# Slabs on two sets of PSUM banks, with the other stages laid into them, in a decoder block on one core

## Chip, core and metric

One NeuronCore of a Trainium2 chip. The metric is device time in microseconds (us) of one execution; lower is better. TensorE does matmuls and transposes into PSUM (eight banks of 128 x 512 f32), ScalarE and VectorE read PSUM, GpSimdE works on SBUF and issues the gathers, SyncE issues the other loads.

## What is computed

One layer, 256 tokens (two blocks of 128), width 2048, all in f32:

```python
h = rmsnorm(x, norm1_w)
q, k, vr, gr, pin, gates = split(h @ w_in)             # 1024, 1024, 2048, 2048, 1024, 4096 columns
ret = silu(gr) * groupnorm(retention(rotary(q), rotary(k), vr))
pooled = (multiscale_pool(pin) @ w_pool_lin) * pool_scale
mixed = sigmoid(gates[0]) * (ret @ w_ret_o) + sigmoid(gates[1]) * (pooled @ w_pool_o)
x = x + mixed @ w_out
h2 = rmsnorm(x, norm2_w)
s = (h2 @ w_q) . sub_keys                              # 8 heads x 2 x 128 keys
# top 16 of each half, top 16 of their 256 sums: 16 experts of 16384 a head and token
a = u[expert] . h2 ; y = sum(gelu(a) * softmax(best) * v[expert])
out = rmsnorm(x + y, final_norm_w)
```

## The kernel before

**Slabs.** All big products run as 19 slabs of 1024 output columns for 256 tokens: 7 of w_in for the mixers (`S_MIX` 0 to 6), 4 for the gates (`S_GATE` 7 to 10), then two each for w_ret_o (`S_RET`), w_pool_o (`S_POOL`), w_out (`S_OUT`) and w_q (`S_Q`). A slab has 16 tiles of 128 rows of weights (8 in `S_POOL`), 288 in all. To keep f32 precision each tile and each activation is split into a high fp32r part and a low rest: SyncE loads `w_raw` (`slab_tiles`, L357), ScalarE rounds it to `w_hi` (`tiles`, L663), VectorE subtracts to `w_lo` (L877), and TensorE does three matmuls for each of four banks (L430 to L432), twelve a tile. `w_raw`, `w_hi` and `w_lo` are rings of `W_RING` = 4 tiles; ScalarE and VectorE run `LEAD` = 3 tiles ahead.

**PSUM.** All slabs write the same four banks, `bank`. The other four, `misc`, serve everything else. So the first matmul of a slab waits (`bank_free`) for the eviction of the slab before it: ScalarE evicts the mix slabs (L706), the gates (L745) and q (L771), VectorE the others (L972, L978, L986). A slab ends with a `drain`.

**What stands between slabs.** Each product needs its activations with the model dimension on partitions. `turn` (L439 to L450) does this in 32 transposes of 128 x 128, in eight groups, through `misc`; each group is evicted as a high part by ScalarE (L678) and a low part by VectorE (L886). `turn` runs four times, each time as a block ahead of a slab: stage 0 ahead of slab 0, on x times norm1_w (L913); stage 1 ahead of `S_RET`; stage 2 ahead of `S_OUT`; stage 3 ahead of `S_Q`, on h2 = x times norm2_w (L991). Between slab 6 and the gates stand the retention (L460 to L491) and the pooling (L497 to L511).

**First gate slab.** Beside it VectorE takes the group norm's statistics (L942, L945) and 16 normalisations in one piece (L956), ScalarE the silu, with fixed numbers of tiles between these blocks (`EARLY` = 4). GpSimdE multiplies (L1210), and later adds the two branches of `mixed` (L1217).

**Keys and top-k.** Behind each `S_Q` slab q is evicted (L771), transposed (L541), split again (L776, L998) and multiplied with the keys (L551 to L553, 24 matmuls for each token block); ScalarE copies the scores (L781). `top_experts(u)` (L1027 to L1059) finds the 16 experts of unit u, one of 16 units (token block and head), on VectorE. `next_tile` (L1023) puts a tile of the second `S_Q` slab between its steps and between the first dot products.

**Experts.** The upper half of each u row is gathered: GpSimdE issues 256 indirect loads of 512 KB (L1235, ring of four), VectorE multiplies each with h2 (`dot_product`, L1066), with `top_experts` of the later units and `q_low(1)` (L998) at fixed places between them. The lower half is done densely: SyncE streams all of u's lower half (L391), TensorE multiplies it in 128 keys of 16 matmuls (L568), ScalarE copies it to `plane` (L800), and later the entries wanted are picked from it by one-hot matmuls (L585, L593) and VectorE (L1128). These picks begin in the middle of the dots: `softmax_and_picks` (L1101) is called before dot 213. Then come the weights, their spreading to the dense keys (L625), the dense product with v's lower half (L641) beside 256 gathers of v's upper half that VectorE adds (L1152), and the final norm.

The order on each engine is the order in which the code issues it; semaphores tie the engines together. Most slabs are hardware loops (`Fori`).

## Time and profile before

| | us |
|---|---|
| median of 3 runs | 2248.27 (2241.54 to 2249.14) |
| span of the profiled execution | 2236.2 |
| TensorE matmuls busy | 2010.6 (90%) |
| VectorE busy | 1359.9 (61%) |
| ScalarE busy | 785.5 (35%) |
| GpSimdE busy | 759.5 (34%) |
| chain that ended last | PE 40%, DMA 25%, DVE 16%, issue 9% |

```profile
PE   6999999899999988899999988179876999999993
PEclk9999999999999999899999999689877899999997
DMA  6766662466564545889989899855677899999996
```

Each digit is a fortieth of the span, 55.9 us, in tenths. PE, PEld, DVE, ACT, POOL and SP are TensorE's matmuls, its weight loads, VectorE, ScalarE, GpSimdE and SyncE; the chip's record of the granted TensorE clock is in tenths of full speed. Matmul records overlap, since a matmul's record holds its tail: the pace is read from start to start. The slabs fill slices 1 to 16, the dense dots slices 17 to 25, the picks and the spreading slices 26 to 32, the dense product with v the rest.

### The profile page before, as it was taken

The numbers are of one execution on the slowest core, as the hardware profiler recorded it, in microseconds if no ns is written. First come the engines' busy times: TensorE is split into PE (matmuls) and PEld (weight loads), VectorE is DVE, ScalarE is ACT, GpSimd is POOL, SyncE is SP. The second block draws the span as 40 slices with busy tenths as digits, with TensorE's granted clock in tenths as the row PEclk, the third lists the DMA queues.
The fourth block names the chain that finished last, engine by engine and source line by source line (L and its number), as shares of the span: only waits on it lengthen the run. The fifth ranks groups of instructions, "written<-read, shape, count | busy, mean of one in ns | idle before, by whom it ended". The sixth has DMA issues, their size and how long they took to land.

```text
span 2236.2 us, 30445 instructions
## 1 busy us (share of the span) xinstructions
PE 2010.6 (90%) x8262; PEld 1515.3 (68%) x8262; DVE 1359.9 (61%) x2570; ACT 785.5 (35%) x1409; POOL 759.5 (34%) x642
## 2 busy tenths in 40 slices
PE   6999999899999988899999988179876999999993
PEld 5878887688787877788888877168765544444441
DVE  4554443644455455876776755579999655554556
ACT  4444445444434353211111111089899411111111
POOL 0340000100002001344443455578654554555453
PEclk9999999999999999899999999689877899999997
DMA  6766662466564545889989899855677899999996
GB/s 214 245 186 189 189 191 61 157 191 188 169 205 155 191 146 163 292 314 327 335 310 320 314 359 342 288 174 173 209 230 226 283 358 371 363 369 355 369 370 220
DMA packets 173711, 565.12 MB, mean 253 GB/s; under 512 B 19296, under 2 KB 20960, under 8 KB 172512
## 3 DMA queue, kind: packets, MB, share of 16 engines
q1 hardware_dynamic: 99936, 296.14, 39.9%
q0 software_dynamic: 73728, 268.47, 34.7%
q8 instruction: 16, 0.26, 0.0%
q14 instruction: 31, 0.25, 0.0%
HBM read 562.43 MB, written 2.10 MB: 252 GB/s over the span
## 4 chain that ended last, share of the span: by engine, by line
PE 40%; DMA 25%; DVE 16%; issue 9%; ACT 5%; POOL 3%; ACTq 0%; POOLq 0%; DVEq 0%; SPq 0%
DMA v_room<-in_peer_v_up,idx 14%; DMA v_room<-in_peer_u_up,idx 11%; PE bank L430 11%; PE bank L431 10%; PE bank L432 10%; DVE v_room L1066 4%; PE misc L593 4%; DVE x_sb L1152 2%; ACT qk_tmp L806 2%; POOL v_room L1235 2%; PE misc L625 2%; DVE w_lo L877 1%; ACT qk_tmp L811 1%; DVE qk_tmp L1012 1%; PE misc L585 1%
## 5 line engine op out<-in xcount | busy, mean ns | idle before, releaser
L877 DVE TENSOR_TENSOR w_lo<-w_raw,w_hi 128x1024 fp32r<-128x1024 f32 x288 | 370.1, 1288 | 385.8 <-ACT w_hi L663 385.2
L663 ACT ACTIVATE w_hi<-w_raw 128x1024 fp32r<-128x1024 f32 x288 | 305.0, 1060 | 466.8 <-PE bank L432 432.5
L1152 DVE SCALAR_TENSOR_TENSOR x_sb<-v_room,weight,x_sb 128x1024 f32<-128x1024 f32 x256 | 328.3, 1283 | 220.4 <-DMA v_room<-in_peer_v_up,idx 217.2
L430 PE MATMUL bank<-w_hi,act_hi 128*128 128x512 f32 x1088 | 428.8, 394 | 28.5 <-DVE w_lo L877 13.4
L641 PE MATMUL bank<-h,qk_tmp 128*128 128x512 f32 x1024 | 439.6, 592 | 0.0
L431 PE MATMUL bank<-w_lo,act_hi 128*128 128x512 f32 x1088 | 426.0, 392 | 0.0
L432 PE MATMUL bank<-w_hi,act_lo 128*128 128x512 f32 x1088 | 425.8, 391 | 0.0
L1066 DVE CUSTOM_DVE_ANT_0 v_room<-v_room,h 128x1024 f32<-128x1024 f32 x256 | 310.2, 1224 | 179.9 <-DMA v_room<-in_peer_u_up,idx 178.4
L1235 POOL DMA_INDIRECT v_room<-in_peer_u_up,idx x256 | 308.2, 1204 | 326.2 <-DVE dots_now L1066 264.2
L1235 POOL DMA_INDIRECT v_room<-in_peer_v_up,idx x256 | 303.9, 1187 | 309.6 <-DVE x_sb L1152 264.1
L641 PEld LDWEIGHTS bank<-h,qk_tmp 128*128 128x128 f32 x1024 | 194.6, 190 | 244.9 <-issue 244.9
L568 PE MATMUL bank<-final_w,h 128*128 128x256 f32 x1280 | 289.2, 383 | 15.3 <-DMA h<-in_peer_u_low 15.2
L568 PEld LDWEIGHTS bank<-final_w,h 128*128 128x128 f32 x1280 | 241.7, 191 | 58.6 <-DMA h<-in_peer_u_low 19.8
L430 PEld LDWEIGHTS bank<-w_hi,act_hi 128*128 128x128 f32 x1088 | 206.0, 189 | 77.8 <-DVE w_lo L877 14.7
L432 PEld LDWEIGHTS bank<-w_hi,act_lo 128*128 128x128 f32 x1088 | 205.9, 189 | 43.5
L431 PEld LDWEIGHTS bank<-w_lo,act_hi 128*128 128x128 f32 x1088 | 206.2, 189 | 42.2
L800 ACT ACTIVATE plane<-bank 128x256 f32 x128 | 49.2, 384 | 414.7 <-PE bank L568 384.0
L855 ACT ACTIVATE qk_tmp<-plane 128x256 f32 x128 | 53.3, 419 | 375.8 <-PE bank L641 366.5
L568 PE MATMUL bank<-final_w,t_extra 128*128 128x256 f32 x768 | 169.7, 379 | 0.0
L568 PEld LDWEIGHTS bank<-final_w,t_extra 128*128 128x128 f32 x768 | 145.9, 190 | 19.8
L625 PE MATMUL misc<-probs_picks,qk_tmp 128*128 128x128 f32 x512 | 107.2, 375 | 43.5 <-ACT qk_tmp L811 41.1
L625 PEld LDWEIGHTS misc<-probs_picks,qk_tmp 128*128 128x128 f32 x512 | 91.9, 270 | 58.9 <-ACT qk_tmp L811 55.9
(167 smaller groups left out, 1565.2 us busy)
## 6 DMA issues: line engine op xcount, KB each, us to landing
w_raw<-in_w_in SPq DMA_DIRECT2D x176, 512.0 KB, 3.6
h<-in_peer_v SPq DMA_DIRECT2D x128, 512.0 KB
h<-in_peer_u_low SPq DMA_DIRECT2D x160, 256.0 KB
t_extra<-in_peer_u_low SPq DMA_DIRECT2D x96, 256.0 KB
w_raw<-in_w_ret_o SPq DMA_DIRECT2D x32, 512.0 KB, 3.8
w_raw<-in_w_out SPq DMA_DIRECT2D x32, 512.0 KB, 3.7
w_raw<-in_peer_w_q SPq DMA_DIRECT2D x32, 512.0 KB, 3.8
w_raw<-in_w_pool_o SPq DMA_DIRECT2D x16, 512.0 KB, 4.7
```

The lines of the kernel that those rows point to most:

```text
L430: pe.matmul(o, lh, rh, start=(k == 0), stop=False)
L431: pe.matmul(o, lh, rl, start=False, stop=False)
L432: m = pe.matmul(o, ll, rh, start=False, stop=(k == kc - 1))
L568: m = pe.matmul(bank[:, n, 0:SEQ], t_ring[r][:, k * P:(k + 1) * P], h2_t[:, s * LOW_KC // 2 + k, :], start=(s == 0 and k == 0), stop=(s == ...
L593: i = pe.matmul(misc[:, 2 + m, n * P:(n + 1) * P], keys_t[:, m, n * P:(n + 1) * P], plane[:, :, bass.ds(g * GROUP + n, 1)].rearrange("p k ...
L625: m = pe.matmul(misc[:, q, n * P:(n + 1) * P], second_hot[:, q % 2, n * P:(n + 1) * P], first_hot[:, q % 2, n, :], start=True, stop=True)
L641: m = pe.matmul(bank[:, 2 * b + h, :], staged[:, r, b * P:(b + 1) * P], e_ring[:, r, h * HALF:(h + 1) * HALF], start=False, stop=False, sk ...
L663: act.activation(w_hi[:, r, :], w_raw[:, r, :], ACT.Copy).then_inc(tile_hi, 1)
L877: dve.tensor_tensor(w_lo[:, r, :], w_raw[:, r, :], w_hi[:, r, :].bitcast(F32), ALU.subtract)\
L1066: dve.tensor_tensor_reduce(out=g_ring[:, r, :], in0=g_ring[:, r, :], in1=h2[:, b, HALF_D:D], scale=1.0, scalar=0.0, op0=ALU.mult, op1=ALU.add,
L1152: dve.scalar_tensor_tensor(acc, g_ring[:, r, :], weight[:, bass.ds(u, 1), k:k + 1].rearrange("p u k -> p (u k)"), acc, ALU.mult, ALU.add). ...
L1235: pool.indirect_dma_start(out=g_ring[:, r, :], out_offset=None, in_=table, in_offset=bass.IndirectOffsetOnAxis(ap=idx[:, m, k:k + 1], axis=0),
```

## The change

- `bank` and `misc` become two equal sets of four banks. Slab s writes `sets[set_of(s)]`, in turn, and waits for that set alone (`set_free[0]`, `set_free[1]` instead of `bank_free`). A set that is free in between takes transposes. The `drain` goes: ScalarE waits for `bank_full` of the slab before it refills the ring slot of the slab's last tile.
- The transposes of all four stages go into slabs, a group of four transposes between one or two tiles. A group now holds two 128-blocks of columns for both token blocks, as the contraction wants them, and a tile waits only for its own group. Stage 0 and 3 transpose x itself; norm1_w and norm2_w, transposed once by TensorE into `norm_t`, are multiplied in as the evictions' scale. x comes in two loads.
- In the first gate slab tiles stand between each two steps of the statistics and the normalisation on VectorE and between the silus on ScalarE.
- The adds of the two branches move from GpSimdE to VectorE, into the evictions of the `S_POOL` slabs (`mix`).
- The first `S_Q` slab's q is transposed after three tiles of the second, its keys are scored after six and seven; top-k of unit 0 starts in that slab. The second slab's q is transposed after two dense keys and scored after eight. `q_low(1)` moves from behind the 15th to behind the 13th dot.
- Constants load one by one between tiles of slab 1; the rotation's table goes ahead. All slab loops are unrolled.

The core of the diff, with the same helpers for ScalarE and VectorE left out where they mirror TensorE's order:

```diff
+def set_of(slab):
+    return (slab + (slab >= S_GATE)) % 2
...
         def _(sp):
-            sp.dma_start(x_sb[:, :, :], a["x"].rearrange("(t p) d -> p t d", p=P)).then_inc(x_landed, 16)
-            sp.dma_start(norm1, a["norm1_w"].rearrange("(o d) -> o d", o=1).to_broadcast([P, D])).then_inc(norm1_landed, 16)
+            sp.dma_start(x_sb[:, :, 0:SLAB], x_rows[:, :, 0:SLAB]).then_inc(x_landed, 16)
...
+            slab_tiles(a["w_in"], 0, 0, 0, LEAD)
+            sp.dma_start(x_sb[:, :, SLAB:D], x_rows[:, :, SLAB:D]).then_inc(x_rest_landed, 16)
...
+            def slab(s, k0, k1, hi, lo):
+                out_set, n, t0, kc = sets[set_of(s)], uses_before(s), first_tile(s), tiles_of(s)
...
                             if k == 0:
-                                pe.wait_ge(bank_free, 4 * s + b + 1)
-                            o = bank[:, b, :]
+                                pe.wait_ge(set_free[set_of(s)], 4 * n + b + 1)
+                            o = out_set[:, b, :]
...
-                    (pe.drain() if k == kc - 1 else m).then_inc(split_free, 1)
+                    if k < kc - 1:
+                        m.then_inc(split_free, 1)
...
+            turn(0, x_sb, misc)
+            turn(1, x_sb, misc)
+            for g in range(8):
+                act_slab(0, 0, 2 * g, 2 * g + 2)
...
+                    turn(g + 2, x_sb, misc)
...
+            for g in range(8):
+                slab(S_RET - 1, 2 * g, 2 * g + 2, act_hi, act_lo)
...
+                turn(g, ret_rows, bank)
+            for b in range(BANKS):
+                pe.wait_ge(turned_lo, 8 + 4 + b + 1)
+            act_slab(S_RET, 1, 0, KC)
...
+            slab(S_POOL + 1, 0, 4, pact_hi, pact_lo)
+            pe.wait_ge(mixed_ready, BANKS)
+            for g in range(4):
+                turn(g, rows, bank)
+                slab(S_POOL + 1, 4 + g, 5 + g, pact_hi, pact_lo)
...
+            act_slab(S_OUT, 2, 0, 4)
+            pe.wait_ge(mixed_ready, 2 * BANKS)
+            for g in range(4, 8):
+                turn(g, rows, misc)
+                act_slab(S_OUT, 2, g, g + 1)
...
+            act_slab(S_OUT + 1, 2, 0, 4)
+            pe.wait_ge(set_free[0], 4 * uses_before(S_Q) + 4)
+            for g in range(4):
+                turn(g, x_sb, bank)
+                act_slab(S_OUT + 1, 2, 4 + 2 * g, 6 + 2 * g)
...
+            act_slab(S_Q, 3, 0, 4)
+            pe.wait_ge(set_free[1], 4 * uses_before(S_Q + 1) + 4)
+            for g in range(4, 8):
+                turn(g, x_sb, misc)
+                act_slab(S_Q, 3, g, g + 1)
+            act_slab(S_Q, 3, 8, KC)
...
+            act_slab(S_Q + 1, 3, 0, 3)
+            pe.wait_ge(set_free[0], 4 * (uses_before(S_Q) + 1) + 4)
+            turn_q(0, bank)
+            act_slab(S_Q + 1, 3, 3, 6)
...
+            score_keys(0, bank)
+            act_slab(S_Q + 1, 3, 6, 7)
+            score_keys(1, bank)
+            act_slab(S_Q + 1, 3, 7, KC)
...
+            dense_dots(0, 0, 0, T_RING)
+            dense_dots(0, 1, 0, T_RING)
...
+            turn_q(1, misc)
...
+            for n in range(BANKS):
+                dense_dots(1, n, 0, T_RING)
+            pe.wait_ge(q_lo, 8)
+            score_keys(0, misc)
+            score_keys(1, misc)
...
         def _(act):
...
+                    r, last = t % W_RING, t - W_RING
+                    if last in LAST_TILES:
+                        act.wait_ge(bank_full, 4 * LAST_TILES.index(last) + 4)
+                    elif last >= 0:
+                        act.wait_ge(split_free, last + 1 - sum(n < last for n in LAST_TILES))
...
+            q_evict(0)
+            tiles(t_q + KC + LEAD, t_q + KC + 7)
+            q_high(0)
+            tiles(t_q + KC + 7, t_q + KC + 10)
+            copy_scores(0, 0)
+            copy_scores(0, 1)
+            tiles(t_q + KC + 10, t_q + 2 * KC)
...
         def _(dve):
...
             for n in range(2 * HEADS):
                 t, h = n // HEADS, n % HEADS
                 m = dve.bn_stats(stat[:, n, :], rows[:, t, V0 + h * DV:V0 + (h + 1) * DV])
+                if n % 2:
+                    tiles(t_gate + LEAD + 2 + n // 2, t_gate + LEAD + 3 + n // 2)
...
+                m = dve.tensor_scalar(y, y, mean_var[:, n, 0:1], norm_a[:, n:n + 1], ALU.subtract, ALU.mult)
...
+                if n < KC - LEAD:
+                    tiles(t_gate + KC + LEAD + n, t_gate + KC + LEAD + n + 1)
...
-            left = list(range(LEAD, KC))
+            left = list(range(t_q + KC + 10, t_q + 2 * KC))
...
                                      top_val[:, 1, :].unsqueeze(1).to_broadcast(grid), ALU.add))
+                next_tile()
                 two_rounds(st, [(cand, best[:, :], best_pos[:, :])], [tmp_a[:, 0:TOPK * TOPK]])
                 next_tile()
...
-            tiles(first_tile(S_Q), LEAD, EARLY)
-            norm_factor(3, 2, 1)
-            tiles(first_tile(S_Q), LEAD + EARLY, KC - EARLY)
             q_low(0)
+            tiles(t_q + KC + 7, t_q + KC + 10)
             top_experts(0)
...
-                    if (u, k) == (0, TOPK - 2):
+                    if (u, k) == (0, 12):
                         q_low(1)
```

## Rows read from the trace of the kernel before

**Rows 1.** Timeline of TensorE, a boundary and a whole slab: start us, us, what.

```profile
70.94 0.39 PE L432 MATMUL bank<-w_hi,act_lo 128*128 128x512 f32 x1
72.07 0.49 PE L430 MATMUL bank<-w_hi,act_hi 128*128 128x512 f32 x1 [0.74 <-ACT rows L706]
...
815.37 0.50 PE L430 MATMUL bank<-w_hi,act_hi 128*128 128x512 f32 x1 [1.67 <-DVE act_lo L886]
...
858.79 0.39 PE L432 MATMUL bank<-w_hi,act_lo 128*128 128x512 f32 x1
```

**Rows 2.** Page, groups by line: busy us, mean ns | idle us before, releaser.

```profile
L877 DVE TENSOR_TENSOR w_lo<-w_raw,w_hi 128x1024 fp32r<-128x1024 f32 x288 | 370.1, 1288 | 385.8 <-ACT w_hi L663 385.2
L663 ACT ACTIVATE w_hi<-w_raw 128x1024 fp32r<-128x1024 f32 x288 | 305.0, 1060 | 466.8 <-PE bank L432 432.5
```

**Rows 3.** Sums of two windows, then the first slab's start on TensorE (timeline).

```profile
core 0: us, PE busy (x) PEld busy (x) DVE busy (x) ACT busy (x) POOL busy (x), PEclk, DMA share, GB/s
3.00:12.00 9.00, 0.00 (x0) 0.00 (x0) 1.02 (x1) 1.03 (x1) 0.00 (x0) 1.00 1.00 413
1800.00:1900.00 100.00, 100.00 (x235) 44.27 (x234) 52.57 (x41) 12.15 (x29) 50.12 (x43) 1.00 0.98 365
...
27.54 0.49 PE L430 MATMUL bank<-w_hi,act_hi 128*128 128x512 f32 x1 [1.70 <-DVE act_lo L886]
```

**Rows 4.** First gate slab: VectorE, TensorE; window (us, busy, clock, DMA share, GB/s).

```profile
400.76 9.69 DVE L956 TENSOR_SCALAR rows<-rows,mean_var,norm_a 128x256 f32<-128x256 f32 x16
...
416.35 0.80 PE L430 MATMUL bank<-w_hi,act_hi 128*128 128x512 f32 x1 [7.50 <-DVE w_lo L877]
...
416.00:422.00 6.00, 5.65 (x13) 0.50 0.74 247
```

**Rows 5.** Transposes ahead of S_RET, S_OUT and S_Q: timeline of TensorE, and one window.

```profile
563.49 0.39 PE L432 MATMUL bank<-w_hi,act_lo 128*128 128x512 f32 x1
564.36 1.94 PE L449 MATMUL misc<-ident_sb,rows 128*128 128x128 f32 x16 [0.49 <-issue]
...
570.87 0.49 PE L430 MATMUL bank<-w_hi,act_hi 128*128 128x512 f32 x1 [1.96 <-DVE act_lo L886]
...
704.35 0.39 PE L432 MATMUL bank<-w_hi,pact_lo 128*128 128x512 f32 x1
...
712.44 0.79 PE L430 MATMUL bank<-w_hi,act_hi 128*128 128x512 f32 x1 [1.70 <-DVE act_lo L886]
...
758.58 0.49 PE L430 MATMUL bank<-w_hi,act_hi 128*128 128x512 f32 x1 [0.75 <-DVE x_sb L986]
...
801.99 0.39 PE L432 MATMUL bank<-w_hi,act_lo 128*128 128x512 f32 x1
...
806.00:814.00 8.00, 6.33 (x32) 0.66 0.00 0
```

**Rows 6.** Around the end of the first S_Q slab: timeline of TensorE and VectorE.

```profile
863.14 0.33 PE L551 MATMUL misc<-keys_hi,pact_hi 128*128 128x128 f32 x1 [1.90 <-DVE pact_lo L998]
...
867.13 0.49 DVE L1007 MAX8 top_val<-scores 128x8 f32<-128x128 f32 x2 [4.05 <-ACT scores L781]
...
878.67 0.17 DVE L1058 SCALAR_TENSOR_TENSOR expert<-expert_ab 128x16 uint32<-128x16 f32 x1
...
885.16 1.23 DVE L1066 CUSTOM_DVE_ANT_0 v_room<-v_room,h 128x1024 f32<-128x1024 f32 x1 [6.31 <-DMA v_room<-in_peer_u_up,idx]
...
887.58 0.80 PE L430 MATMUL bank<-w_hi,act_hi 128*128 128x512 f32 x1 [5.18 <-DVE w_lo L877]
```

**Rows 7.** Waits of TensorE: us in total, times, longest us.

```profile
PE misc L585 <- POOL second_bf L1254: 58.0, 3, 54.9
```

**Rows 8.** Windows, L1066 alone: us, VectorE busy (records), clock, DMA share, GB/s.

```profile
931.00:1261.00 330.00, 131.24 (x220) 0.98 0.90 318
1300.00:1400.00 100.00, 52.73 (x87) 1.00 0.98 351
1407.00:1452.00 45.00, 27.14 (x45) 0.56 0.81 272
```

More of the change, by code:

```diff
@@ L760, in _ @@
[L760 to L767 removed]
+            tiles(t_gate + KC, t_gate + KC + LEAD)
+            evict(S_GATE, ACT.Sigmoid)
+            for s in range(S_GATE + 1, S_RET - 1):
+                tiles(first_tile(s) + LEAD, first_tile(s + 1) + LEAD)
+                if s == S_GATE + V0 // SLAB:
+                    act.wait_ge(ret_ready, NB)
+                evict(s, ACT.Sigmoid)
@@ new lines, in _ @@
+            gate_ret(S_RET + 1)
+            t_mix = first_tile(S_POOL + 1)
+            tiles(gate_wait + 2 * KC, t_mix + LEAD)
+            mix(S_POOL)
+            tiles(t_mix + LEAD, t_mix + 7)
+            for g in range(4):
+                turned_low(2, g, bank)
+                tiles(t_mix + 7 + g, t_mix + 8 + g)
+            mix(S_POOL + 1)
+            t_out = first_tile(S_OUT)
+            tiles(t_out + LEAD, t_out + 7)
+            for g in range(4, 8):
+                turned_low(2, g, misc)
+                tiles(t_out + 3 + g, t_out + 4 + g)
@@ new lines, in _ @@
+            t_out += KC
+            tiles(t_out - KC + 11, t_out + LEAD)
+            add_resid(S_OUT)
+            tiles(t_out + LEAD, t_out + 7)
+            for g in range(4):
+                turned_low(3, g, bank)
+                tiles(t_out + 7 + 2 * g, t_out + 9 + 2 * g)
+            t_q = first_tile(S_Q)
+            tiles(t_out + 15, t_q + LEAD)
+            add_resid(S_OUT + 1)
+            tiles(t_q + LEAD, t_q + 7)
+            for g in range(4, 8):
+                turned_low(3, g, misc)
+                tiles(t_q + 3 + g, t_q + 4 + g)
```

542 lines of the change are left out of this document (303 added, 239 removed).

## Prediction

> **What bounds the kernel now.** I read the page's busy times and its slices first. TensorE leads there, but that is a mean over two unlike halves, so I went on by stages: the timeline of TensorE, the waits, and sums of windows.
>
> Up to about 940 us TensorE sets the pace. In a slab its 192 matmuls start 0.227 us apart (815.37 to 858.79 is 191 steps, [rows 1]), twelve to a tile, so a tile takes 2.72 us and a slab 43.5. Beside that a tile costs 1.06 us on ScalarE and 1.29 on VectorE [rows 2]: both have room, as long as nothing else sits in their queue. What TensorE loses lies between the slabs: 1.13 us instead of 0.227 at a plain boundary, since the next slab waits for the eviction of the same banks [rows 1]; a start at 27.54 us [rows 3]; 7.5 us in the first gate slab [rows 4]; the transposes before S_RET, S_OUT and S_Q [rows 5]; and the key scores and top-k around the two S_Q slabs [rows 6].
>
> From about 880 to 1463 us TensorE is no longer the bound. The waits say it plainly: TensorE sits 54.9 us before the first key turn (L585), for keys that come only when the 212th gathered row has been multiplied, and `softmax_and_picks` has run behind it [rows 7]. Its 2048 dense dots end 55 us too early. The stream of gathers on VectorE (L1066) needs 330 us for 110 dots while top-k lies between them, 3.0 us each (two records a dot), about 2.3 later and 2.0 with the dense loads gone [rows 8]. After 1463 each step waits for the one before; from 1800 TensorE is 100% busy and the DMA engines 0.98 [rows 3], and all of it hangs on the picks. **So the end moves by as much as the 212th dot moves**, and that starts with the first top-k (done 878.85, first dot 885.16, [rows 6]).
>
> The profiled span is 2236.2 us; the median of the three runs, 2248.27, is 12.1 above it. I take the gain off both alike.
>
> **The change part by part.** First the time of the last matmul of the first S_Q slab, before 858.79 + 0.23 = 859.0 [rows 1].
>
> *Start.* The multiply by norm1 and the wait for 3 MB go; only 1 MB of x, the identity and two small tables are waited for. Data moved at 413 GB/s from 3 to 12 us [rows 3], so 1 MB is there at about 5.6 and the small ones at 6.3. Then one transpose, eight more at the half clock (2 x 0.113 each, below), a tile on ScalarE and VectorE and the first group's eviction: first matmul at about 10.8, bounds 9 and 15. Against 27.54 that is 16.7 less. The other 24 transposes now lie inside the slab, at 0.113 each in a row of 28 or 32 with a warm clock (16 took 1.94 us, some 0.2 of it the last one's tail, [rows 5]): 2.7 back. The first twelve matmuls may run at 0.427 instead of 0.227, as they do behind the gate stall [rows 4]: 2.4 back. Gain 11.6. The second half of x (1 MB, 2.5 us more) is needed only after six tiles.
>
> *Plain boundaries.* 13 of them (six in the mix slabs, three in the gates, RET to RET, RET to POOL, POOL to POOL, OUT to OUT) lose 1.13 - 0.227 = 0.90 each. The other set has been evicted a slab ago, so all goes: 11.7. The drain goes too; ScalarE now waits for the last bank of the slab before it refills that tile's slot, which leaves it 3 tiles or 8.2 us, for 2.4 us of eviction and one tile. Hidden; without that cover it would cost about 1 us per slab.
>
> *First gate slab.* VectorE runs 16 normalisations in one piece, 9.69 us, and the tiles behind them come late: 7.50 us idle, then 6 us at granted clock 0.50 with 13 matmuls, 12 of them 0.427 apart [rows 4]. That is 7.7 from start to start, 12 x 0.2 = 2.4, and 0.2 on the first. With a tile between each two steps VectorE has 0.6 + 1.29 us of work per 2.72 us, so the stall goes: 10.3.
>
> *Transposes.* 32 inside slabs cost 32 x 0.113 = 3.6 us. Before S_RET the way from last to next start was 7.38 us, less 0.23; the last group's eviction still stands before the slab (1.96 us, same banks): gain 7.15 - 3.6 - 1.9 = 1.6. Before S_OUT 8.09 us, and the slab behind it takes 46.14 to the next one's start where 43.5 and a boundary, 44.5, would do, 1.6 more [rows 5]: 7.9 + 1.6 - 3.6 = 5.8. Before S_Q 13.38 us (801.99 to 815.37, [rows 1, 5]), most of it the wait for norm2 and transposes partly at the half clock: 13.15 - 3.6 = 9.5. The adds that move from GpSimdE to VectorE (eight of about 0.6 us) fit between its tiles: a POOL slab has 22 us, its eight tiles 10.
>
> Sum: 11.6 + 11.7 + 10.3 + 1.6 + 5.8 + 9.5 = 50.5. The first S_Q slab ends at 808.5.
>
> *First top-k.* Here the interleaving costs. Before, key scores followed the slab at once and the top-k was done 19.8 us behind its end. Now, counted from that end T: three tiles (8.2), the transposes (to 10.1), three tiles (18.3), the first 24 key scores at 0.113 (21.0), then 1.3 to the first MAX8 as in the rows (24 scores end 865.8, MAX8 at 867.13, [rows 6]): T + 22.3. The top-k itself is 11.7 us including two tiles; now three tiles stand in it, and the first (tile 10 of the second S_Q slab) comes from ScalarE only after the second copy of scores, T + 28.8, so about 4 us are waited. Done at about T + 38, bounds T + 31 (no waiting) and T + 46 (each of its three tiles waits a whole tile time). That is 18.3 us later than before, and takes back 18.3 of the 50.5: first top-k at 846.6, 32.2 us earlier. Behind it on VectorE stands tile 13: it follows the first dot, T + 44.4, so TensorE should idle some 4 us there and restart with 12 slow matmuls. The old kernel has that too (5.18 us before 887.58, [rows 6]). It delays only TensorE, which has 55 us to give and gets more.
>
> *Gathers.* Eight dense keys now stand ahead of the second half's key scores; `q_low(1)` comes at the 13th dot, about T + 79, when its transposes (about T + 67) are done, so VectorE should not wait. In the first unit ten tiles less lie between the dots. They are worth at most 12 us by VectorE's time, nothing where the gather itself is late (a pace of 2.3 with the dense loads beside it, [rows 8]); I take 1. The dense dots end about 66 us earlier, the gathers only 32, so some 30 us more of them run at 2.0 instead of 2.3: 2.4. Gain at the 212th dot: 32.2 + 1 + 2.4 = 35.6.
>
> *SyncE's queue.* The constants no longer load in one block before the second slab's tiles but one behind each two of them. Each waits in that queue for a tile's slot; the first to need one is the rotation on GpSimdE, whose table goes ahead in the first slab, the others follow after 300 us: 0, and if a tile came late it would be by one load, up to 3 us once.
>
> *Unrolled loops.* More instructions are fetched. The S_Q slabs were straight code before and kept 0.227, so 0; up to 3 us if every slab paid one loop's restart.
>
> 2236.2 - 35.6 = 2200.6 of span, and **2213 us** as median, 1.6% faster.
>
> **A rule against the change.** At 806 us TensorE began transposing at the half clock, and the transposes themselves brought it back: nothing else ran on it until the slab at 815.37, which started at full speed; the granted clock over that stretch is 0.66 [rows 1, 5]. The Trainium skill, page "TensorE: Matmul & The Clock Gate", section "Part 4: PE-mode transpose", says that transposes do not count as busy for the clock in the same way. By that rule, transposes spread through slabs would cool them; this trace speaks against it, though it never shows transposes between matmuls.
>
> **The rivals.** *Gathers run ahead:* the ten tiles taken from the first unit were in the way, or the top-k comes at T + 31. Then up to 9 us more: 2204. For: VectorE took dots and tiles in turn there, 1.2 us each. Against: dots with no tile between them keep 3.0 [rows 8].
>
> *The mixed slabs stall:* 5 slabs with transposes, squares, adds or the first start lose 2 to 3 us each to the four-tile ring, some with the slow restart: 13 us less, 2226. For: late tiles cost 10.3 us at one place in [rows 4]. Against: each queue holds at most 3 us of other work between two tiles, and the ring gives 5 of slack.
>
> *Slower: the clock.* 39 tiles lie between transposes. At the half clock a tile costs 12 x 0.2 = 2.4 us more, 94 us for all: 2213 + 94 = 2307. It outweighs the gain from 15 cold tiles on, where the result is 2248; below that it only trims.
>
> **How the numbers follow.** Forecast (2205 to 2221) 0.53; gathers ahead 0.17; stalls 0.18; clock 0.12, half of it about even, half slower. The range 2194 to 2235 takes in the first three with the bounds of start and top-k, and leaves out the clock and some tail. About 0.5% (11 us) can be told from no change: faster 0.88, same 0.06, slower 0.06.
>
> **What would show it.** First slab matmul near 11 us; slab to slab 0.23 us apart; no gap over 1 us in the first gate slab; 1.9 us before S_RET and none before S_OUT and S_Q; first S_Q slab ending near 808; first top-k near 847 and first dot near 853; TensorE idle some 85 us before L585 at about 1427. I am wrong if the first top-k is within 20 us of its old time, if the matmuls between transposes start 0.427 apart, or if the dots run slower than 3.0 us once dense dots lie beside them.

## The result, and the profile after

| | before | after |
|---|---|---|
| median | 2245.48 us (4 runs, 2241.54 to 2249.14) | 2187.52 us (4 runs, 2186.43 to 2193.35) |
| profiled execution: span / time | 2236.2 / not recorded | 2186.4 / 2188.32 |
| TensorE waits before the first key turn | 54.9 us | 82.3 us |
| first slab matmul | 27.54 | 11.99 |
| transposes of the first `S_Q` slab's q | 859.29 | 816.03 |
| first top-k done / first dot | 878.8 / 885.2 | 845.8 / 852.0 |
| dot 16 / 128 / 208 / 212 | 931.4 / 1271.3 / 1451.9 / 1461.1 | 894.1 / 1234.6 / 1407.2 / 1416.5 |
| first add of a v row, start / last, end | 1605.0 / 2219.1 | 1559.3 / 2169.3 |

Dots are counted from 0 at the first; dot 212, called the 212th below, is the first behind `softmax_and_picks`. The waits of TensorE and the profiled execution belong to one execution each.

The ratio is 0.9755, 95% interval 0.9733 to 0.9776. The direction was right, the size was not: 2213 was forecast, with 2194 to 2235 as the range, and 2187.5 lies 6.5 us below its lower end.

The page of the kernel after, its span, engines, slices (now 54.7 us each) and groups, to be read beside [rows 2]:

```profile
span 2186.4 us, 28606 instructions
PE 1990.6 (91%) x8263; PEld 1506.8 (69%) x8263; DVE 1361.6 (62%) x2592; ACT 787.4 (36%) x1430; POOL 745.8 (34%) x634
...
PE   8999999999999999999999984099777999999994
PEclk9999999999999999999999997599777999999997
DMA  6766662665555556998998899756677899999996
...
L1004 DVE TENSOR_TENSOR w_lo<-w_raw,w_hi 128x1024 fp32r<-128x1024 f32 x288 | 373.0, 1298 | 317.4 <-ACT w_hi L741 315.5
...
L741 ACT ACTIVATE w_hi<-w_raw 128x1024 fp32r<-128x1024 f32 x288 | 305.2, 1061 | 366.6 <-PE bank L445 194.1
```

From the second slice to the 23rd TensorE has nothing below a 9, where before dipped four times; ScalarE and VectorE do the same tiles at the same price. The hole in slices 25 and 26 is TensorE, done early, waiting for the dots.

Its timeline on TensorE, start and duration in us, in five groups: a slab boundary (the answer to 70.94 and 72.07 in [rows 1]), the start ([rows 3]), the way into `S_RET` ([rows 5]), q's transposes inside the second `S_Q` slab, and tile 13 ([rows 6]).

```profile
60.88 0.39 PE L445 MATMUL bank<-w_hi,act_lo 128*128 128x512 f32 x1
61.11 0.39 PE L443 MATMUL misc<-w_hi,act_hi 128*128 128x512 f32 x1
...
11.99 0.79 PE L443 MATMUL bank<-w_hi,act_hi 128*128 128x512 f32 x1 [2.61 <-DVE act_lo L1017]
...
536.47 0.60 PE L462 MATMUL bank<-ident_sb,rows 128*128 128x128 f32 x4
538.74 0.47 PE L443 MATMUL bank<-w_hi,act_hi 128*128 128x512 f32 x1 [1.68 <-DVE act_lo L1012]
...
816.03 1.91 PE L590 MATMUL bank<-ident_sb,q_rows 128*128 128x128 f32 x16
817.69 0.48 PE L443 MATMUL misc<-w_hi,act_hi 128*128 128x512 f32 x1
...
854.40 0.80 PE L443 MATMUL misc<-w_hi,act_hi 128*128 128x512 f32 x1 [3.79 <-DVE w_lo L1004]
```

The next slab starts 0.23 us behind the last matmul. No two starts are more than 0.32 us apart from 359.1 (the first gate slab, where [rows 4] show 7.50 us of idling in before) to the last of the transposes ahead of `S_RET`, and none from 538.74 to 850. Two sums of windows of the same kernel (each engine's busy us, then the granted clock):

```profile
core 0: us, PE busy (x) PEld busy (x) DVE busy (x) ACT busy (x) POOL busy (x), PEclk, DMA share, GB/s
358.00:495.00 137.00, 137.00 (x606) 113.46 (x606) 83.28 (x110) 68.42 (x72) 9.42 (x2) 1.00 0.62 187
806.00:847.00 41.00, 41.00 (x214) 35.04 (x214) 23.77 (x49) 19.26 (x23) 0.19 (x1) 1.00 0.53 176
```

The granted clock stays at 1.00, that is 2.4 GHz, with transposes (and key scores) between the matmuls.

### The profile page after: what moved, and what is told of

It reads as the page before. It is cut to its first block, busy times and chain, and to the rows that moved or that the text cites. A ratio compares the mean times of both kernels' runs of the same rounds, so it can differ in the third digit from the quotient of the medians.

```text
span 2186.4 us, 28606 instructions
## 1 busy us (share of the span) xinstructions
PE 1990.6 (91%) x8263; PEld 1506.8 (69%) x8263; DVE 1361.6 (62%) x2592; ACT 787.4 (36%) x1430; POOL 745.8 (34%) x634
## 3 DMA queue, kind: packets, MB, share of 16 engines
q0 software_dynamic: 73728, 268.47, 35.6%
## 4 chain that ended last, share of the span: by engine, by line
PE 44%; DMA 25%; DVE 15%; issue 9%; ACT 3%; POOL 3%; DVEq 0%; ACTq 0%; POOLq 0%; SPq 0%
DMA v_room<-in_peer_v_up,idx 14%; DMA v_room<-in_peer_u_up,idx 10%; PE bank L443 6%; PE bank L445 6%; PE bank L444 6%; PE misc L443 5%; PE misc L445 5%; PE misc L444 5%; DVE v_room L1250 5%; PE misc L667 5%; DVE x_sb L1334 3%; POOL v_room L1410 3%; ACT qk_tmp L933 2%; PE misc L699 2%; DVE qk_tmp L1194 1%
## 5 line engine op out<-in xcount | busy, mean ns | idle before, releaser
L443 PE MATMUL bank<-w_hi,act_hi 128*128 128x512 f32 x576 | 227.2, 394 | 4.3 <-DVE act_lo L1017 2.6
L445 PE MATMUL bank<-w_hi,act_lo 128*128 128x512 f32 x576 | 225.5, 392 | 0.0
L444 PE MATMUL bank<-w_lo,act_hi 128*128 128x512 f32 x576 | 225.3, 391 | 0.0
L443 PE MATMUL misc<-w_hi,act_hi 128*128 128x512 f32 x512 | 202.1, 395 | 3.8 <-DVE w_lo L1004 3.8
L444 PE MATMUL misc<-w_lo,act_hi 128*128 128x512 f32 x512 | 200.5, 392 | 0.0
L445 PE MATMUL misc<-w_hi,act_lo 128*128 128x512 f32 x512 | 200.5, 392 | 0.0
L901 ACT ACTIVATE plane<-bank 128x256 f32 (+1 forms) x128 | 49.0, 383 | 410.3 <-PE bank L625 410.3
L1402 POOL COPY idx<-expert 128x16 uint32 (+1 forms) x32 | 10.6, 332 | 402.9 <-DVE expert L1242 402.7
```

The lines of the kernel that those rows point to most:

```text
L443: pe.matmul(o, lh, rh, start=(k == 0), stop=False)
L444: pe.matmul(o, lh, rl, start=False, stop=False)
L445: m = pe.matmul(o, ll, rh, start=False, stop=(k == kc - 1))
```

## The experiments

Stages below are starts in us from the span's start, read from the timeline of one execution of each kernel. The kernels ran in three groups, each on a chip of its own together with the kernel before: `before_again`, `one_set`, `fillers` and `thin`; `after_again`, `drain`, `early` and `split`; `after_third`, `hold`, `turns24` and `early_split`. The first group has no repeat of after, so its three changed kernels are compared with after across chips. `before_again`, `fillers`, `thin` and `turns24` have one execution each, so their times carry no spread.

### The same kernels again

`before_again`: the kernel before, unchanged.

> The kernel before, unchanged, profiled a second time. The profiled execution of it spanned 2236.2 us and its timed runs took 2241.5 to 2249.1, while the changed kernel's execution took 1.9 us more than its span. Theory A (executions of the kernel before differ by up to 10 us, and the differences lie where 128 x 4 KB gathers run beside dense loads): the first S_Q slab ends at 859 within 1 us again, the first dot at 885 within 1 us, and the later stages spread by several us. Theory B (some 10 us lie around the span in the kernel before and not in the changed one): span 2236 again, and the time about 10 us above it.

`after_again` and `after_third`: the kernel after, unchanged.

> The changed kernel, unchanged, again: a baseline on this chip and the spread of its stages. Slab stages within 0.3 us of 816.0 at the first q transpose, first dot 852; what differs lies behind dot 16 and in the 256 added rows (610 us in the first profile, 615 in the kernel with the boundary waits).

> The changed kernel, unchanged, as the baseline of this chip: median 2187 to 2193, slabs and first dot as before (816.0, 852), the stages behind dot 128 spread by some 6 us.

| | before | before again | after | after again | after third |
|---|---|---|---|---|---|
| span / its time | 2236.2 / - | 2243.0 / 2244.75 | 2186.4 / 2188.32 | 2194.8 / 2196.78 | 2189.4 / 2191.30 |
| q transposes | 859.29 | 861.37 | 816.03 | 815.84 | 816.18 |
| first dot | 885.2 | 889.9 | 852.0 | 852.1 | 852.2 |
| dot 128 | 1271.3 | 1276.6 | 1234.6 | 1235.0 | 1235.6 |
| dots 128 to 208 | 180.6 | 180.7 | 172.6 | 177.7 | 174.8 |
| adds, first to last | 614.1 | 615.4 | 610.0 | 612.5 | 609.2 |

An execution's time is 1.8 to 2.0 us above its span, not 12.1. Three profiled executions of after agree to 0.4 us up to the first dot and to 1 us at dot 128, and part only behind it. The two of before do not agree: q's transposes come 2.1 us later in the second and the first dot 4.8, where 1 was expected. Most of that is TensorE at 1.2 GHz in places where the first execution had 2.4. The first slab starts with eight matmuls about 0.427 apart, which is 1.7 us; the first `S_RET` slab does too, while the first `S_OUT` slab, slow in the first execution (46.14 us, [rows 5]), runs at full speed. And the second half of the 48 key scores starts 0.213 apart, not 0.111. Timeline of `before_again`, TensorE and then VectorE:

```profile
867.62 0.27 PE L551 MATMUL misc<-keys_hi,pact_hi 128*128 128x128 f32 x1
867.73 0.28 PE L552 MATMUL misc<-keys_lo,pact_hi 128*128 128x128 f32 x1
...
868.24 0.41 PE L552 MATMUL misc<-keys_lo,pact_hi 128*128 128x128 f32 x1
868.45 0.41 PE L553 MATMUL misc<-keys_hi,pact_lo 128*128 128x128 f32 x1
...
875.46 1.23 DVE L877 TENSOR_TENSOR w_lo<-w_raw,w_hi 128x1024 fp32r<-128x1024 f32 x1 [3.30 <-ACT w_hi L663]
```

The scores take 2.4 us more for it, ScalarE copies them later, and the tile that stands in the first top-k waits 3.30 us behind that copy. In after the scores lie among matmuls and start 0.11 apart in all three executions. So the profile that the forecast read was a quick one of before even ahead of the first gather. Executions of before ranged from 2238.5 to 2253.0 in one group and from 2234.9 to 2249.7 in another. So the 12.1 us between the profiled span of before and its median were mostly the distance between a quick execution and the middle one; and that median, 2248.27 of three runs, lies above the medians of all four comparisons (2240.92 to 2245.48). After against before in the two later groups: medians 2192.02 and 2240.92, ratio 0.9771 [0.9746, 0.9795]; 2194.93 and 2244.10, ratio 0.9793 [0.9764, 0.9822]. The gain is 49 us by these and 58 by the first comparison.

### What the plain boundaries had cost

`one_set`: at each of the 13 plain boundaries TensorE waits for the eviction of the slab before it, bank by bank, as if both slabs wrote the same banks.

```diff
+                plain = s in (1, 2, 3, 4, 5, 6, 8, 9, 10, 12, 13, 14, 16)
...
                                 pe.wait_ge(set_free[set_of(s)], 4 * n + b + 1)
+                                if plain:
+                                    pe.wait_ge(set_free[set_of(s - 1)], 4 * (uses_before(s - 1) + 1) + b + 1)
```

> The changed kernel with the 13 plain boundaries undone: the first matmul on each bank of these slabs also waits for the eviction of the same bank of the slab before it. Theory A (gathers set the end, and they start where the slabs let them): boundaries lose 0.7 to 0.9 us each again, the first S_Q slab ends 9 to 12 us later, the first dot too, and the end 9 to 12 us later, about 2198. Rival (TensorE's slack before the key turn covers it): first dot later, end within 3 us.

`drain`: the two sets stay, and the `drain` at the slab's end comes back in the same 13 places.

```diff
                     if k < kc - 1:
                         m.then_inc(split_free, 1)
+                    elif s in (0, 1, 2, 3, 4, 5, 7, 8, 9, 11, 12, 13, 15):
+                        pe.drain()
```

> The changed kernel with the drain of TensorE put back at the end of the 13 slabs that have a plain boundary behind them; both sets stay. The eviction waits alone, put back, cost 0.18 us a boundary (first q transpose 2.3 us later), not the 0.90 of the old kernel. Theory A (the drain and the restart behind it were the other 0.7): first q transpose 8 to 10 us later, about 825, and first dot and end with it. Rival (the hardware loop's branch was it): less than 2 us later.

| | after again | one_set | drain |
|---|---|---|---|
| q transposes | 815.84 (others 816.03, 816.18) | 818.32 | 822.75 |
| median us, ratio to before | 2192.02, 0.9771 [0.9746, 0.9795] | 2197.80, 0.979 [0.9757, 0.9824] | 2200.72, 0.982 [0.9801, 0.984] |

Timeline of TensorE in `drain`, the first boundary:

```profile
61.06 0.39 PE L445 MATMUL bank<-w_hi,act_lo 128*128 128x512 f32 x1
61.67 0.47 PE L443 MATMUL misc<-w_hi,act_hi 128*128 128x512 f32 x1 [0.22 <-issue]
```

From last to first start that is 0.61 instead of 0.227, 0.08 more to the second matmul, and some 0.04 over the next ten: 0.50 a boundary (a mix slab takes 44.02 us from start to start instead of 43.52), 6.5 for 13. The q transposes come 6.6 to 6.9 later, between the two expectations. The wait for the same banks costs less, and not everywhere: nothing at the six mix boundaries and at two gates, 0.68 at the first of the three gates' boundaries (401.13), 0.54 at each of the four where VectorE evicts (581.83, 625.99, 648.40, 718.28), and some 0.1 behind each of these five: together 3.4. The q transposes come only 2.1 to 2.5 later, because in this execution the first slab had fewer slow matmuls and ended 1.0 earlier; neither expectation came true. The ScalarE timeline of `one_set` shows why a mix boundary is free:

```profile
101.05 1.06 ACT L744 ACTIVATE w_hi<-w_raw 128x1024 fp32r<-128x1024 f32 x1 [1.66 <-PE misc L448]
102.01 2.44 ACT L765 ACTIVATE rows<-misc,row_scale 128x512 f32<-128x512 f32 x4
```

Bank 0 is full nine matmuls before the slab's end, and its eviction, 0.61 us of the 2.44, is over at 102.6, 1 us before the next slab starts (103.57). The kernel before did the same (four evictions in 2.53 us from 158.77, the slab's last matmul at 160.10, the next slab at 161.20). Only at the boundary of [rows 1] did ScalarE begin late, at 71.17, so that bank 0 was free at about 71.8 for a slab that started at 72.07. Nor does the trace of before show the banks as the last to come where VectorE evicts. Its VectorE, then its TensorE, behind the first `S_RET` slab, whose last matmul starts at 614.30:

```profile
614.25 2.47 DVE L972 TENSOR_TENSOR rows<-rows,bank 128x512 f32 x4
...
615.43 0.49 PE L430 MATMUL bank<-w_hi,act_hi 128*128 128x512 f32 x1 [0.74 <-DVE rows L972]
```

One eviction takes 0.62, so bank 0 is free at about 614.9, and the slab starts 0.5 later. Before lost much the same at all 13 boundaries, 0.84 to 0.93 from start to start (`before_again` 0.87 to 0.99), and 1.0 a slab with the matmuls behind it (44.5 us against 43.52), whichever engine evicts. The drain gives half of that, 0.50; the other half, some 0.5 at each boundary, has no shown cause. All 13 stood at the turn or the end of a hardware loop in before and none does in after; whether a loop's restart is the rest was not tried, nor drain and bank wait together. Behind the q transposes the loss can't be followed: `one_set` has its 212th dot at 1421.0, the repeats of after at 1422.2 and 1420.1, `drain` at 1424.9; of the ratios `drain`'s stands apart from that of after on the same chip, and `one_set` has no such neighbour.

### Do transposes cool the clock?

`turns24`: the four transposes of group 3 ahead of `S_RET` are issued 24 times, 96 in a row between two tiles of the last gate slab.

```diff
-            def turn(g, src, out_set):
+            def turn(g, src, out_set, times=1):
 
-                for c in range(2):
+                for c in [0, 1] * times:
...
-                turn(g, ret_rows, bank)
+                turn(g, ret_rows, bank, 24 if g == 3 else 1)
```

> The changed kernel with one group of four transposes in the last gate slab issued 24 times, 96 transposes in a row, for nothing but the time. Theory A (transposes keep the clock up as matmuls do, as at 806 us in the kernel before): they start 0.109 to 0.113 us apart to the last, 10.5 us in all, the granted clock stays 1.00, and the matmuls behind them start 0.227 apart; everything behind is 10.3 us later. Rival (transposes do not count as activity): within the 96 their distance doubles to about 0.21, and the first matmuls behind start 0.427 apart.

Timeline of TensorE, then its sums by window (us, TensorE busy, granted clock, DMA share, GB/s):

```profile
511.77 10.64 PE L462 MATMUL bank<-ident_sb,rows 128*128 128x128 f32 x96
522.17 0.48 PE L443 MATMUL misc<-w_hi,act_hi 128*128 128x512 f32 x1
522.48 0.40 PE L444 MATMUL misc<-w_lo,act_hi 128*128 128x512 f32 x1
522.71 0.39 PE L445 MATMUL misc<-w_hi,act_lo 128*128 128x512 f32 x1
...
512.00:516.00 4.00, 4.00 (x39) 1.00 0.49 154
516.00:520.00 4.00, 4.00 (x39) 1.00 0.00 0
520.00:524.00 4.00, 4.00 (x31) 1.00 0.00 0
```

96 transposes take 10.40 us from the first start to the next matmul's, 0.108 each, at granted clock 1.00, and the matmuls behind them start 0.23 apart at once. Everything behind is 10.0 us late by it, 92 added transposes at 0.109; the q transposes come 8.9 late (825.11), because in this execution the first slab's slow matmuls ended 1.1 us sooner. The time, 2204.09, is 9.2 above `after_third`'s median. The Trainium skill's rule (page "TensorE: Matmul & The Clock Gate", section "Part 4: PE-mode transpose": transposes do not count as busy for the clock in the same way) would have had these matmuls start at the low clock; nothing of it shows here for these f32 transposes, which the profile lists as MATMUL. Each added transpose simply costs its 0.11 us.

### Do tiles between the first dots delay the gathers?

`fillers`: in after three tiles stand behind the first dot, in before eleven. Here eight VectorE operations of a tile's size (1024 columns, to a buffer that is not in use) go back into the places of the missing eight.

```diff
+            fill = [8]
+
             def next_tile():
...
                     tiles(t, t + 1)
+                elif fill[0]:
+                    fill[0] -= 1
+                    step(dve.tensor_tensor(probs_picks[:, :], x_sb[:, 0, 0:SLAB], x_sb[:, 1, 0:SLAB], ALU.subtract))
```

> The changed kernel with eight more VectorE instructions of a tile's size (1.2 us, 1.4 with their own wait) in the first unit, where the old kernel had eight more tiles: behind the fourth and fifth dot, two in the second top-k, four behind dots six to nine. Theory A (those tiles stood in the way of the dots, which is why dot 16 gained 4 us more than dot 0): dot 16 comes 4 to 8 us later than in the changed kernel, 898 to 902, and the end as much. Rival (the gathers pace the first unit, the 4 us come from the TensorE stall or the loads): dot 16 at 894 within 1 us.

The first dot stays (852.1). Dot 8 comes at 883.4 instead of 873.1, dot 16 at 900.0 instead of 893.2 to 894.1, dot 64 at 1043.9 instead of 1037.4 to 1038.0, dot 212 at 1425.5 instead of 1416.5 to 1422.2; time 2199.18. So what stands between the first dots delays them, by 6 to 7 us at dot 16; at dot 128 some 5 us are left (1240.3 against 1234.6 to 1235.6), and at dot 212 3 to 9. In before dot 16 came 46.2 and 46.7 us behind dot 0, in after 41.1 to 42.1: 4 to 5.5 us gained there, where I took 1.

### Contention of the dense loads with the gathers

`thin`: the dense loads carry a quarter of their bytes, each into the first quarter of its buffer, and the dense matmuls read that quarter alone. It leaves out three quarters of u's lower half, so its dot products are not the right ones.

```diff
-                            sp.dma_start(t_ring[r], a["peer_u_low"][:, bass.ds((BANKS * i + n) * SLAB + s * HALF, HALF)])\
+                            sp.dma_start(t_ring[r][:, 0:HALF // 4],
+                                         a["peer_u_low"][:, bass.ds((BANKS * i + n) * SLAB + s * HALF, HALF // 4)])\
...
-                        m = pe.matmul(bank[:, n, 0:SEQ], t_ring[r][:, k * P:(k + 1) * P], h2_t[:, s * LOW_KC // 2 + k, :],
+                        m = pe.matmul(bank[:, n, 0:SEQ], t_ring[r][:, 0:P], h2_t[:, s * LOW_KC // 2 + k, :],
```

> The changed kernel with a quarter of each load of u's lower half (512 bytes of each 2 KB row), the dense matmuls all reading that quarter; the lower half of the dot products is not computed rightly. Number and pace of matmuls stay. Theory A (dense loads and gathers share the DMA engines, and that alone makes a gathered dot take 2.3 instead of 1.94 us): dots 128 to 176 take 1.9 to 2.0 us each instead of 2.3, 15 us less; dots 16 to 128, between which top-k lies, fall from 3.03 to 2.8 or less. Rival (from dot 16 to 128 the top-k steps and the ring of four set the pace, not the loads): 3.03 stays there within 0.05, and only the later dots gain.

`hold`: the dense product stops behind its first keys until the 32nd dot, so that as many loads beside the dots come later instead.

```diff
             score_keys(1, misc)
+            pe.wait_ge(g_free, AHEAD + G_RING + 32)
```

> The changed kernel with the dense dots held from key 8 on until 32 gathered dots are done (about 940), some 40 us; TensorE then ends them at about 1378, 45 us ahead of the picks still. Theory A (dense loads slow the gathers, a dot takes 2.3 us beside them and 1.94 without, so ending them earlier is what the dots behind number 128 gained): dots 16 to 32 run faster (2.8 instead of 3.0), dots behind 172 slower, the 212th dot 2 to 6 us later than in the unchanged kernel. Rival (TensorE's end of the dense dots has nothing to do with it): 212th dot as in the baseline within its spread, and dots 176 to 208 at 1.94 though dense loads lie beside them.

| us a dot | after, again, third | thin | hold |
|---|---|---|---|
| 16 to 128 | 3.04, 3.05, 3.05 | 2.83 | 3.03 |
| 128 to 176 | 2.30, 2.41, 2.34 | 2.10 | 2.29 |
| 176 to 208 | 1.94, 1.93, 1.96 | 1.99 | 2.23 |
| dense products end | 1335.0 to 1341.8 | 1322.3 | 1376.0 |
| dot 212 | 1416.5 to 1422.2 | 1382.8 | 1422.2 |

The dense loads slow the gathers by 0.2 to 0.3 us a dot in both of the first stages. With a quarter of the bytes left dots 128 to 176 still take 2.10, where 1.9 to 2.0 was expected. Without three quarters of their bytes the 212th dot comes 34 to 39 us earlier and the time falls to 2159.43. `hold` shows the other half: with TensorE held (it waits 39.6 us at its dense matmul) and the loads pushed back, the last dots run at 2.23 instead of 1.94, because the dense products now end at 1376 and not 1335 to 1342. Dots 16 to 128 win 2.9 us by it, the 32 dots from 176 on lose 8.7, and the 212th dot comes 2.1 us later than in `after_third`; medians 2200.52 and 2194.93, ratios 0.9808 [0.9776, 0.9839] and 0.9793 [0.9764, 0.9822], too close to call. In these two kernels the loads' bytes are paid wherever they lie. That confirms the term "30 us more of the dots run at the quicker pace" in kind.

### The first top-k earlier

`early`: in the second `S_Q` slab q is transposed after one tile instead of three, its keys are scored after three and four instead of six and seven, and TensorE's, ScalarE's and VectorE's orders follow; the tiles left for the dots are brought forward.

```diff
-            act_slab(S_Q + 1, 3, 0, 3)
+            act_slab(S_Q + 1, 3, 0, 1)
             pe.wait_ge(set_free[0], 4 * (uses_before(S_Q) + 1) + 4)
             turn_q(0, bank)
-            act_slab(S_Q + 1, 3, 3, 6)
+            act_slab(S_Q + 1, 3, 1, 3)
...
-            act_slab(S_Q + 1, 3, 6, 7)
+            act_slab(S_Q + 1, 3, 3, 4)
             score_keys(1, bank)
-            act_slab(S_Q + 1, 3, 7, KC)
+            act_slab(S_Q + 1, 3, 4, KC)
```

> The changed kernel with q of the first S_Q slab transposed after one tile of the second instead of three, keys scored after three and four tiles instead of six and seven, and ScalarE's and VectorE's tiles put around that; three tiles stand ready before the first dot. Theory A (the first top-k sets the gathers, they set the end): first top-k about 12 us earlier, 834, first dot about 840, the 3.8 us wait of TensorE ahead of tile 13 gone, and the end 10 to 13 us earlier than the changed kernel on this chip. Rival (the loads set the end and take the gain back): first dot 840, end within 4 us of the changed kernel's.

VectorE's timeline, the end of the first top-k and the first dot of `early`, then the same two of after:

```profile
833.20 0.17 DVE L1242 SCALAR_TENSOR_TENSOR expert<-expert_ab 128x16 uint32<-128x16 f32 x1
...
842.60 1.23 DVE L1250 CUSTOM_DVE_ANT_0 v_room<-v_room,h 128x1024 f32<-128x1024 f32 x1 [3.96 <-DMA v_room<-in_peer_u_up,idx]
```

```profile
845.59 0.17 DVE L1242 SCALAR_TENSOR_TENSOR expert<-expert_ab 128x16 uint32<-128x16 f32 x1
...
851.98 1.23 DVE L1250 CUSTOM_DVE_ANT_0 v_room<-v_room,h 128x1024 f32<-128x1024 f32 x1 [6.21 <-DMA v_room<-in_peer_u_up,idx]
```

The top-k is done 12.4 us earlier, but the first dot only 9.4: its row takes 9.4 us from the experts to the dot instead of 6.4. Of the 3.0 us more, 0.6 lie ahead of the first gather's issue (2.5 us behind the experts instead of 1.9) and 2.4 between its issue and its dot (6.9 instead of 4.5). SyncE's timeline in `early` shows what went beside it, tiles of the slab and then the dense product's loads:

```profile
830.58 8.41 SPq L369 DMA_DIRECT2D w_raw<-in_peer_w_q  x4
839.37 2.60 SPq L404 DMA_DIRECT2D h<-in_peer_u_low  x4
842.22 2.48 SPq L404 DMA_DIRECT2D t_extra<-in_peer_u_low  x4
```

Three tiles (1.5 MB, issued at 834.5, 836.0 and 838.7) and the first eight dense loads (2 MB, from 839.4 on) share the DMA engines with the first four gathers (835.7 to 839.8). In after the last tile had landed at 844.2, the dense loads went out from 840.2 on, and four of the eight had landed when the first gather was issued at 847.5. That the loads cause the longer way is the likely reading; no run moved them alone. Some 8 us of the lead last (dot 128 at 1227.0 against 1234.6 to 1235.6), and the medians are 2186.69 and 2192.02, ratios 0.9757 [0.9739, 0.9776] and 0.9771 [0.9746, 0.9795]; these overlap, so that the end bears the gain out only in size (5.3 us, between the two expectations), not beyond doubt. The place of the key scores in the slab is worth what it moves the first dot; it was right to charge it.

### What sets 3.0 us a dot

In after's timeline one unit's top-k stands on VectorE in one piece, and a gather can only be issued when a slot of the ring of four comes free (VectorE, then GpSimdE):

```profile
1072.79 1.22 DVE L1250 CUSTOM_DVE_ANT_0 v_room<-v_room,h 128x1024 f32<-128x1024 f32 x1 [0.91 <-DMA v_room<-in_peer_u_up,idx]
...
1082.37 0.18 DVE L1242 SCALAR_TENSOR_TENSOR expert<-expert_ab 128x16 uint32<-128x16 f32 x1
...
1091.61 1.23 DVE L1250 CUSTOM_DVE_ANT_0 v_room<-v_room,h 128x1024 f32<-128x1024 f32 x1 [4.39 <-DMA v_room<-in_peer_u_up,idx]
```

```profile
1076.00 0.96 POOL L1410 DMA_INDIRECT v_room<-in_peer_u_up,idx  x1 [0.97 <-POOL idx L1402]
1084.50 1.14 POOL L1410 DMA_INDIRECT v_room<-in_peer_u_up,idx  x1 [7.54 <-DVE dots_now L1250]
```

Top-k holds VectorE from the end of the first dot shown to 1082.5, some 8.5 us; GpSimdE issues no gather for 8.5 us (1076.00 to 1084.50), and after four dots on the rows at hand VectorE stands 4.4 us for the next. `split` cuts each unit's top-k in three parts with dots between them; nothing else changes but the places of the parts.

```diff
                 next_tile()
+                yield
...
-                    if found < UNITS and (k in (4, 12) and u or (u, k) == (0, 4)):
-                        top_experts(found)
-                        found += 1
+                    if k in (1, 4, 6, 9, 12, 14) and u or (u, k) in ((0, 3), (0, 5), (0, 7)):
+                        next(parts)
```

> The changed kernel with each top-k cut into three parts that stand apart between the dots, instead of 8.2 us in one piece twice a unit. From dot 16 to 128 a dot takes 3.03 us, 2.83 with thin dense loads; VectorE has 17.4 us of work in each 24.3. Theory A (one piece of 8.2 us lets the ring of four run full and stand still, and behind it VectorE waits for the refill): pace 2.4 to 2.6, dot 128 some 50 to 70 us earlier, the end 35 to 60 us earlier, unless TensorE's dense dots, done at 1335, then come last and hold the picks. Rival (the DMA engines are the bound, 0.9 busy there): pace 2.9 or more.

`early_split`: both.

> Both edits that helped: q transposed and scored earlier in the second S_Q slab, and each top-k in three parts between the dots. Theory A (the end follows the 212th dot): the gains add but for what the loads take back, 48 and 5 to 8 us against the changed kernel: 2132 to 2142. Rival (in the split kernel TensorE's dense dots or the loads already bound): 2144, as with the split alone.

| | after again / third | split | early_split |
|---|---|---|---|
| us a dot, 16 to 128 | 3.05 / 3.05 | 2.51 | 2.55 |
| dot 212 | 1422.2 / 1420.1 | 1366.1 | 1358.0 |
| median us | 2192.02 / 2194.93 | 2143.94 (2137.46 to 2149.80) | 2130.31 (2128.27 to 2139.38) |
| ratio to before | 0.9771 / 0.9793 | 0.9567 [0.9536, 0.9598] | 0.9507 [0.9479, 0.9536] |

Sums of one window for the dots alone, in after and in `early_split` (us, VectorE busy in dots (records, two a dot), clock, DMA share, GB/s):

```profile
1040.00:1160.00 120.00, 47.31 (x79) 1.00 0.92 325
```

```profile
1040.00:1160.00 120.00, 56.95 (x95) 1.00 0.98 357
```

The DMA engines go from 0.92 to 0.98 and from 325 to 357 GB/s: so the ring and the long top-k, not the DMA engines, held this stage in after, and in `early_split` the DMA engines are the likely next bound, which no run tested. Each of the two kernels ran beside one repeat of after, `split` beside the first and `early_split` beside the third. `split` takes 48 us off it, `early_split` 65: 2.9% below after and 4.9% below before, the quickest kernel here. What `early` adds on top of `split` was not run on one chip; the 212th dot is 8.1 us earlier by it. The time of `early_split`, 2130.31, lies just below the 2132 to 2142 expected.

## Why the prediction was right, and where it was wrong

**The slabs: right to the microsecond, in part by luck.** First slab matmul 11.99 (10.8 was said, bounds 9 to 15). Transposes of q at 816.03, three tiles or 8.2 us behind the slab's end, which puts that at 807.9; 808.5 was said. Slab to slab 0.23, no stall in the first gate slab, 1.68 us ahead of `S_RET` (1.9 was said), none ahead of `S_OUT` and `S_Q`: the rivals of stalling mixed slabs and of a cooler clock are out. Slow matmuls, 0.427 apart, are the first tile's and tile 13's, twelve each, as forecast. Three terms missed and cancelled. The start gave 10.1, not 11.6: 15.5 for the earlier matmul, less the 5.5 us by which the first slab is longer. The plain boundaries gave 13.3, not 11.7, since a slab was 1.0 us too long and not 0.90. And 0.9 came ahead of the first gate slab (36.70 us from the last mix matmul instead of 37.57), where nothing was forecast. The S_OUT term held 1.6 us for a slow restart that `before_again` does not have there.

**The top-k: right.** Done at 845.8 (846.6), first dot 852.0 (853), TensorE 3.79 us idle ahead of tile 13 (4). The wait before the first key turn is 82.3 (85).

**The cause of the loss at a boundary: wrong, near the right size.** [rows 1] name ScalarE's eviction as what ended the last wait, and I took the whole for a wait on the same banks, with the drain hidden. But the drain alone is 0.50 everywhere, the banks cost nothing at eight of the 13 boundaries when put back alone (0.6 to 0.8 at five), and some 0.5 at each has no shown cause. Since the change removes all of it, the sum came out; that is luck in the cause. The step "the drain goes too ... Hidden" was mis-sized: it is worth 6.5 us.

**The gather terms: too small.** From the first dot to the 212th I gave 3.4 us of gain (1 in unit 0, 2.4 for contention); it was 11.4 (44.6 less 33.2), and against `before_again` the two repeats give 6.6 and 8.7. Unit 0 gave 4.1, since tiles between dots are in the way (`fillers`); they were eight fewer, not the ten of the forecast (3 behind the first dot instead of 11). The rival "gathers run ahead" was right in this, and I set it at 0.17 on the ground that dots without tiles keep 3.0. They do, but for another reason, the ring (`split`). It weighs less in unit 0, where one top-k stands among 16 dots and not two. From dot 128 to 208 after took 172.6, 177.7 and 174.8 us against 180.6 and 180.7: 3 to 8, where 2.4 was said. In kind that is the contention of `thin` and `hold`; the profiled execution had it at the upper end.

**The adds: not forecast.** They took 610.0 against 614.1. Repeats of after gave 609.2 and 612.5, `before_again` 615.4, other kernels of this study 610.8 to 615.8 with the same code there; nothing says that the change did it.

**The anchor: the largest single error.** The step that failed is "I take the gain off both alike": it put the 12.1 us between the span of before and its median on top of the forecast span, as a constant distance. A span and its time are 1.9 us apart, and the median of after lies 1.1 above its profiled span; the rest was one quick execution against a median of three, in a kernel whose executions range over 15 us. The sum in this profile's own terms: 2200.6 forecast of span, 2186.4 measured, 14.2 less: 9.0 up to the 212th dot (1.0 at the first dot, 3.1 in unit 0, -0.6 on to dot 128, 5.6 on to dot 208, -0.1 behind it) and 5.2 after that, mostly the adds. The remaining 11.3 of the 25.5 us missed are the anchor. In gain against gain the miss is 13 to 22: 35.6 was forecast, and the three comparisons gave 58, 49 and 49. Against `before_again` 5.6 of it lie ahead of the first dot, which came 37.8 us earlier and not 32.2: mostly the half-clock stretches that the forecast's profile did not have; after has none between its first slab and tile 13. How often the kernel before has them is open, with two profiles of it.

## What to carry to other kernels

Follow the marker that sets the end (here the 212th dot) through each stage, and forecast its shift; before a median is added to a profiled span, see how far a span and its own execution's time lie apart, and widen by the spread of executions instead. Profile the kernel before twice: here the second profile had the first dot 4.8 us later, mostly by slow matmuls that the first did not have. A wait that a profile attributes to one releaser may hide others beneath it: what is removed with it decides the size, not the name; see when that releaser's work was done. Where a ring of a few slots feeds an engine, one long piece of other work on that engine can stop the ring. Cut in three it left 2.51 us a dot, 0.1 to 0.2 above the pace with no top-k (2.30 to 2.41), where it had been 3.05, and here that was worth about as much again as the whole change.

## What the chip showed unexpectedly

- 96 transposes in a row, 10.4 us with no other matmul, kept the granted clock at 1.00, 0.108 us each (`turns24`).
- A `drain` on TensorE between two streams of matmuls costs 0.38 us from start to start and 0.12 over the matmuls behind it (`drain`, the same at all 13 places but one, 0.03 longer).
- The same 48 key scores took 5.3 us in one execution of before and 7.7 in another, where the second 24 started 0.213 apart, at a granted clock of 0.50; among matmuls, in after, they started 0.11 apart in all three.
- The first gathered row took 6.4 us from the experts to its dot in after, and 9.4 with 3.5 MB of direct loads issued beside it and the three gathers behind it (`early`).
- Gathers and dense loads together reach 357 GB/s at a DMA share of 0.98 with the top-k cut in three, and 325 at 0.92 when the ring of four stands still behind 8.5 us of top-k (`early_split`, after).
